# Norm chains through token-major sums, and modulation pieces moved out of the gaps into feed-forward stages

## What is computed

```python
def rms_norm(x, g):
    xf = x.astype(jnp.float32)
    y = xf * lax.rsqrt(jnp.mean(xf * xf, axis=-1, keepdims=True) + RMS_EPS)
    return (y * g.astype(jnp.float32)).astype(x.dtype)
def modulate(x, g_pre, shift, scale):
    return rms_norm(x, g_pre) * (1.0 + scale) + shift
def swiglu(h, w1, w3, w2):
    return (jax.nn.silu(h @ w1) * (h @ w3)) @ w2
def half_ffn(v, shift, scale, gate, g_pre, g_post, w1, w3, w2):
    out = swiglu(modulate(v, g_pre, shift, scale), w1, w3, w2)
    return v + 0.5 * gate * rms_norm(out, g_post)
...
    m_lat = (sc @ w_mod[l] + b_mod[l]).reshape(n_b, N_MOD, 1, D_MODEL)
```

## Time and profile before

| | us |
|---|---|
| median of three runs (2689.0 to 2689.52) | 2689.05 |
| the profiled execution | 2683.14 |
| its span, first to last instruction | 2681.4 |
| PE busy | 2305.6 |
| DVE busy | 1226.1 |
| ACT busy | 816.1 |
| POOL busy | 86.6 |
| mean granted TensorE clock, share of full speed | 0.909 |

### The profile page before, as it was taken

The page is one execution under the profiler, slowest core; times in us unless marked ns, Lnnn a source line. Parts: engine busy times, 40 slices in busy tenths (PEclk is TensorE's granted clock), DMA queues, the critical chain, the costliest instruction groups (busy, mean ns, idle before and its releaser), DMA issues. The chain is left out here.

```text
span 2681.4 us, 29935 instructions
## 1 busy us (share of the span) xinstructions
PE 2305.6 (86%) x12457; PEld 1870.2 (70%) x12457; DVE 1226.1 (46%) x1773; ACT 816.1 (30%) x1248; POOL 86.6 (3%) x99
## 2 busy tenths in 40 slices
PE   4899999799885586899999899999799872877997
PEld 2578888487554575678888578888588551766997
DVE  0422334852546546643334643334644546446555
ACT  1422221532233412242122232222333233313443
POOL 0000000000000310000000000000000000400000
PEclk9899999899787777999999899999889876878998
DMA  7253423422222012342432532432423210025572
GB/s 240 87 144 107 111 75 106 127 89 83 69 63 79 1 48 95 113 107 70 127 89 76 157 89 71 117 97 84 143 73 110 73 63 0 1 63 169 160 196 88
DMA packets 403175, 258.89 MB, mean 97 GB/s; under 512 B 21834, under 2 KB 401760, under 8 KB 403040
## 3 DMA queue, kind: packets, MB, share of 16 engines
q1 hardware_dynamic: 403040, 256.97, 33.0%
HBM read 255.89 MB, written 1.05 MB: 96 GB/s over the span
## 5 line engine op out<-in xcount | busy, mean ns | idle before, releaser
L674 PE MATMUL bank<-uh,wh 128*128 128x512 f32 (+1 forms) x1536 | 565.0, 368 | 38.8 <-DVE ul L1523 25.0
L676 PE MATMUL bank<-uh,wl 128*128 128x512 f32 (+1 forms) x1536 | 558.4, 364 | 0.0
L675 PE MATMUL bank<-ul,wh 128*128 128x512 f32 (+1 forms) x1536 | 558.3, 363 | 0.0
L1468 DVE TENSOR_TENSOR wl<-ring,wh 128x2048 fp32r<-128x2048 f32 (+1 forms) x160 | 323.8, 2023 | 157.2 <-ACT wh L1127 156.4
L1127 ACT ACTIVATE wh<-ring 128x2048 fp32r<-128x2048 f32 (+1 forms) x160 | 270.9, 1693 | 319.4 <-PE bank L676 281.9
L674 PEld LDWEIGHTS bank<-uh,wh 128*128 128x128 f32 x1536 | 293.4, 191 | 99.6 <-issue 41.6
L676 PEld LDWEIGHTS bank<-uh,wl 128*128 128x128 f32 x1536 | 293.6, 191 | 44.9
L675 PEld LDWEIGHTS bank<-ul,wh 128*128 128x128 f32 x1536 | 294.3, 192 | 42.7
L674 PE MATMUL bank<-hh,wh 128*128 128x512 f32 (+1 forms) x704 | 255.4, 363 | 0.0
L675 PE MATMUL bank<-hl,wh 128*128 128x512 f32 (+1 forms) x704 | 255.2, 362 | 0.0
L676 PE MATMUL bank<-hh,wl 128*128 128x512 f32 (+1 forms) x704 | 255.2, 362 | 0.0
(11 more groups left out here) (268 smaller groups left out, 3018.7 us busy)
## 6 DMA issues: line engine op xcount, KB each, us to landing
ring<-in_ffn_w_dram SPq DMA_DIRECT2D x176, 512.0 KB, 5.3
ring<-in_w_mod_dram SPq DMA_DIRECT2D x144, 512.0 KB, 4.6
ring<-in_ffn_w_dram SPq DMA_DIRECT2D x64, 384.0 KB, 3.4
ring<-in_ffn_w_dram SPq DMA_DIRECT2D x64, 320.0 KB, 4.1
ring<-in_w_in_dram SPq DMA_DIRECT2D x40, 512.0 KB, 4.7
ring<-in_w_out_dram SPq DMA_DIRECT2D x16, 512.0 KB, 7.2
ring<-in_w_in_dram SPq DMA_DIRECT2D x4, 544.0 KB, 4.5
ring<-in_w_in_dram SPq DMA_DIRECT2D x2, 1024.0 KB, 5.3
```

The lines of the kernel that those rows point to most:

```text
L674: pe.matmul(bank, w_hi, x_hi, start=first, stop=False)
L675: pe.matmul(bank, w_hi, x_lo, start=False, stop=False)
L676: return pe.matmul(bank, w_lo, x_hi, start=False, stop=last)
L1468: TT(low[:, b, 0:floats], at, high[:, b, 0:floats].bitcast(F32), ALU.subtract).then_inc(wl_ready, 1)
```

## The change

The file has four kinds of edits.

**Where modulation pieces are computed.** The five gap places are gone. There are 9 pieces after up pieces of the first FFN's first part (7 before), 3 after up pieces of its second part, 9 in layer 0's second FFN, 9 in layer 1's first FFN, and 20 and 14 in the mixing blocks (21 and 11 before). In the mixing blocks that is one less at the end of layer 0's, and in layer 1's one more at `mla`, one at `prep` and one at the end.

**The sums and their inverse.** The squares are now the weights of the product and two columns of ones its moving operand: four products of 128 tokens each, two columns wide, per chunk. The sums then lie token by token on the partitions. Root and reciprocal are taken of 128 by 4 values, and `spread` brings the inverse back to 128 by 512 with four products against the identity; DVE reads it from the bank.

**What else a norm chain does.** The gain of postnorm goes to ACT, chunk by chunk while the stage still runs, all but the last before its end; the two gain adds per chunk become one add, and POOL does it for chunks 2 and 5. The last chunk's square goes to PE by itself and not through `yacc`. POOL computes `ul` of the odd chunks, and `wl` of the first piece of each dense stage but the output projection. ACT rounds that first piece at the end of the stage before. `round_in_place` is gone: before `proj` the modulated input is put in a view of the arena and rounded into `uTh` at once.

**The first piece of a stage.** Its 48 products go chunk by chunk over both matrices (in `proj` over both units), so that each chunk of `ul` releases six products and not three.

```diff
-    MOD_PLAN = {("start", 0): 8, ("ffn", 0): 7, ("gap0", 0): 5, ("mix", 0): 21, ("gap1", 0): 5, ("gap2", 0): 5,
-                ("gap0", 1): 5, ("mix", 1): 11, ("gap1", 1): 5}
+    MOD_PLAN = {("start", 0): 8, ("ffn0", 0): 9, ("ffn1", 0): 3, ("mix", 0): 20, ("ffn2", 0): 9,
+                ("ffn0", 1): 9, ("mix", 1): 14}
...
-    MOD_AFTER = {("up0", 0, 0): ("ffn", 0)}
+    MOD_AFTER = {("up0", 0, 0): ("ffn0", 0), ("up1", 0, 0): ("ffn1", 0), ("up0", 0, 1): ("ffn2", 0),
+                 ("up0", 1, 0): ("ffn0", 1)}
...
+        POOL_ADDS = (2, 5)
+        POST_BANK, PRE_BANK, NORM_AT = 5, 4, 56
...
-        MIX_PIECES = ((0, 2, 2, 2, 1, 1, 1, 1, 1, 4), (0, 1, 2, 2, 1, 1, 0, 0, 0, 4))
+        MIX_PIECES = ((0, 2, 2, 2, 1, 1, 1, 1, 1, 3), (0, 2, 2, 2, 1, 1, 1, 0, 0, 5))
...
+            def spread(n, bank, tiles):
+                pe.wait_ge(inverse_ready, n + 1)
+                for i in tiles:
+                    last = pe.matmul(bank[:, i * P:(i + 1) * P],
+                                     rst[:, NORM_AT + i:NORM_AT + i + 1].to_broadcast([P, P]), ident,
+                                     start=True, stop=True)
+                last.then_inc(inverse_spread, 1)
...
+            def token_sums(bank, squares, tiles, first, last):
+                for i in tiles:
+                    done = pe.matmul(bank[:, 2 * i:2 * i + 2], squares[:, i * P:(i + 1) * P], ones[:, 0:2],
+                                     start=first and i == tiles[0], stop=last, skip_group_check=True)
+                return done
...
             def gap(l, j):
-
-                m = gap_pieces(l, j)
-                if m[0]:
-                    mod_work(*m[0])
                 postnorm(l, j)
-                if m[0]:
-                    mod_work(*m[1], banks=(6, 0))
                 if after(l, j)[0] < LAYERS:
                     prenorm(*after(l, j))
-                if m[0]:
-                    mod_work(*m[2])
-                    pe.wait_ge(mod_copied, m[2][0])
...
+                        fresh = part == 0 and j == 0
+                        order = [(g, k) for k in range(KC) for g in range(2)] if fresh else [
+                            (g, k) for g in range(2) for k in range(KC)]
...
+            def split_first(n, floats, parts=(wh, wl)):
+                pool.wait_ge(wh_ready, SPLIT[n] + 1)
+                pool.wait_ge(wl_ready, SPLIT[n])
...
+            def low_rest(l, j, t0, u, high, low):
+                for m in range(1, KC, 2):
+                    pool.wait_ge(uh_ready, split_before(l, j) + m + 1)
+                    G.tensor_tensor(low[:, m, t0:T], u[:, m, t0:T], high[:, m, t0:T].bitcast(F32), ALU.subtract
+                                    ).then_inc(ul_pool, 1)
```

More of the change, by code:

```diff
@@ L636, in mod_work @@
                         mod_turn(g, bank(g))
-            def norm(n, src, blocks, ready, t0):
-                if n:
-                    pe.wait_ge(rms_ready, n)
-                for m in range(blocks):
-                    ready(m)
-                    last = pe.matmul(ps[5][:, t0:T], ones, src(m), start=m == 0, stop=m == blocks - 1)
-                last.then_inc(sums_ready, 1)
-            def prenorm(l, j):
-                t0 = HALF * pre_halves(l, j)[0]
-                norm(6 * l + 2 * j, lambda m: sq[:, m, t0:T], KC,
-                     lambda m: pe.wait_ge(x_squared, 8 * (3 * l + j) + m + 1), t0)
@@ new lines, in token_sums @@
+            def token_sums(bank, squares, tiles, first, last):
[3 more added lines that the diff above has]
+                return done
+            def prenorm(l, j):
+                tiles = tiles_of(pre_halves(l, j))
+                n = 6 * l + 2 * j
+                for m in range(KC):
+                    pe.wait_ge(x_squared, 8 * (3 * l + j) + m + 1)
+                    done = token_sums(ps[PRE_BANK], squares_of(j)[:, m, :], tiles, m == 0, m == KC - 1)
+                done.then_inc(sums_ready, 1)
+                spread(n, ps[PRE_BANK], tiles)
@@ L716, in proj, with product @@
             def proj(l):
-                for n, (kind, j, c0, w, dest) in enumerate(UNITS):
+                def product(n, k):
+                    kind, j, c0, w, dest = UNITS[n]
                     t0 = first_of(l, dest)
@@ L1039, in store @@
             def store():
-                pe.wait_ge(x_ready, 8 * 3 * LAYERS)
+                for m in range(KC):
+                    wait_x(pe, 3 * LAYERS - 1, m)
                 for t in range(2):
@@ L1208, in ffn @@
                             round_piece(PIECES[f"up{part + 1}", l, f][0], 2048)
+                        else:
+                            round_next(l, 2 * f)
+                        if part == PARTS - 1 and j:
+                            gain(l, 2 * f, j - 1, hs)
+                gain(l, 2 * f, KC - 1, hs)
             def proj(l):
@@ L1401, in out_proj @@
                             A(uh[:, m, t0:T], uT[:, m, t0:T], ACT.Copy).then_inc(uh_ready, 1)
+                    for m in range(2 * j - 4, 2 * j - 2):
+                        if m >= 0:
+                            gain(l, 1, m, hs)
+                round_next(l, 1)
+                for m in range(2 * OUT_PIECES - 4, KC):
+                    gain(l, 1, m, hs)
             def store():
@@ L1921, in out_proj @@
                 split_rest(PIECES["out", l][0], 2048)
-                for m in range(KC):
+                for m in range(0, KC, 2):
                     dve.wait_ge(uh_ready, split_before(l, "out") + m + 1)
```

274 lines of the change are left out of this document (161 added, 113 removed).

## The result

| | before | the change |
|---|---|---|
| median of four runs (us) | 2689.03 | 2712.78 |
| lowest and highest | 2670.10 to 2689.52 | 2710.18 to 2716.72 |
| ratio with its 95% interval | | 1.0107 [1.006, 1.0153] |
| profiled execution | 2683.14 | 2714.9 |
| its span | 2681.4 | 2713.1 |

The difference of the two profiled executions is 31.8 us, that of the medians 23.7. The kernel before ran again beside the experiments, with executions from 2680 to 2690 us.

A forecast was written before the change was run, and what follows sets the result against it. PE was busy for 2305.6 of 2681.4 us, so what counted was the gaps between dense stages and what stands there. Pieces +63.4, norm chains -36.4: net +27 us, median from 2689 to 2716, range 2694 to 2729.

The forecast's parts named there:

- The row of pieces: Modulation pieces between up pieces: 23 more pieces and three more first ones, which do not wait, add 63.4 us.
- The 2.92 us: Cost of a modulation piece in a row: 1.07 product, some 0.5 turn, 1.25 waiting for ACT's copy.
- 64 x 0.21 = 13.5 us: Prenorm's token sums in a full gap: 64 narrow passes at 0.21 us, with PE staying at 1.2 GHz.
- The rival from the page's rule: Sustained PE activity raises the clock under the token sums: net -9 us, so 2680; chance 0.09.
- The gaps: Five gaps between dense stages, about 194 us where they were 228; first products 27 to 29 us after the stage.
- The first piece with its hold: First product until PE goes on in a full gap: 14.3 us, the middle of 13.2 and 15.2.
- the upper bound: First piece: POOL's four subtractions of 1.27 us each hold DVE back in full, and PE goes on after 15.2.
- the lower bound: First piece: all 48 products fed together, about 11 at 0.42 and 37 at 0.227 us, make 13.2.
- The modulation pieces in there cost next to nothing where they are.: In the old gaps, pieces standing beside work of DVE and ACT cost next to nothing.
- The start: Start's norm: sums 13.5 for 10, reciprocal and root 0.6 for 4.0, spread +1.9, first piece gains 1.5: 0.
- What was left at nothing: Parts taken at no change, among them the mixing blocks' moved pieces and POOL's hidden split of the first piece.
- Rival 1: Clock rises under the token sums, saving 36 us in gaps and start: net -9, so 2680; chance 0.09.

The follow-up runs named there:

- no_pool: The changed kernel with POOL's two adds and four subtractions of each gap back on DVE; 2710.86 us, ratio 1.0096.
- placement_only: The kernel before with the change's placement of the modulation pieces and nothing of its norm chains; 2729.17 us, ratio 1.0164.
- gaps_again: The changed kernel with its new norm chains, but the modulation pieces where the kernel before had them; 2710.17 us, ratio 1.0085.
- sums_128: The changed kernel with 128 moving columns instead of 2 in each product of the prenorm's token sums; 2686.52 us, ratio 1.0002.
- gaps_128: gaps_again with 128 moving columns in the prenorm's token sums, the edit of sums_128; 2676.66 us, ratio 0.9977.

## Why the prediction was right

- **The row of pieces.** +63.4 forecast, +64.0 measured. The 2.92 us was a period read off the trace in a row with the same queue order, and it holds because that order does not change. Its parts were right too: 1.25 of wait forecast, 1.34 gone when the bank was doubled.
- **The clock in the gap.** "64 x 0.21 = 13.5 us" was 13.8. The step that carried it was to price narrow passes by the products at 2184, which stayed at 0.50 although PE was never idle, and not by the 0.12 they take behind dense work. The rival from the page's rule would have given 2680; the clock did not rise. In the gap at 1530 the errors are small and cancel in part: the sums began at 6.9 us after the stage for 7.8, took 0.3 more than forecast, and ended at 20.7 for 21.3.
- **The gaps.** First products 27.0, 26.7, 27.6, 28.5 and 16.6 us after the stages, forecast 27.1, 27.1, 28.5, 28.5 and 15.5 (order: the gaps at 1115 and 1530, before layer 0's and layer 1's `proj`, with 256 tokens). The first piece with its hold took 14.6, forecast 14.3 as the middle of 13.2 and 15.2. The middle was a choice between two bounds and not worked out: three multiplies were held for 0.94 us each, where the upper bound had four operations of 1.27. no_pool shows the lower bound for what it was, DVE alone: 13.0 to 13.5.
- **"The modulation pieces in there cost next to nothing where they are."** This sentence failed. placement_only shows 12.3 us for 25. It did no harm to the sum, because the new gaps were built up from their own steps and not from the old ones less a saving. But read as "the chains gained 34 us" the sum misleads: 12 of these came from taking the pieces out, 21 from the chains, and gaps_again shows that without the placement the chains lose 22.
- **The start.** 0 forecast (its own terms add to +0.5), +2.6 measured. 2.1 of it is there before the first square: ACT's squares start at 69.38 and not at 67.28, in the set-up that I had not looked at. What delays it was not tried. The norm itself is within 0.5 us.
- **What was left at nothing.** The projections and the last FFN grew by 3.2 us: 1.6 in layer 1's projection, which spent longer at the lower clock (a mean of 0.92 for 0.93), and 1.45 in a wait of a down piece of the last FFN for its low part. The mixing blocks were -1.8 together, -5.9 and +4.1, and the -5.9 is less than they differ by between traces.
- **Rival 1's price.** I gave 36 us to a clock that rises under the sums. sums_128 gave 28 at the start and in the gaps, because the clock is still low for the first 3 to 5 us of them everywhere.

## What to carry to other kernels

Before work is moved beside or away from a chain, find out which engine *is* the chain, before and after the edit: the same five pieces cost 0.5 us each on average beside a chain of DVE and 2.2 each once PE was the chain. A shorter instruction is not a cheaper one if the clock stays down under it: sums with 2 columns moving left PE at 1.2 GHz, and with 64 times the columns they took a third less time. And where a helper is given to every step of a row, look at what the next step waits for in it: a second bank was worth 34.7 us, more than the 33.5 that all edits of the gaps brought.

## What the runs showed of the hardware

- Products with 2 columns moving and 128x128 weights, back to back, took 0.21 us per pass at 1.2 GHz, and the granted clock stayed at 0.50 through 10 us of uninterrupted work; behind dense work they took 0.12. With 128 columns moving the rows of sums in sums_128 started at 0.50 and were at 1.00 3 to 5 us later; in gaps_128 two rows started at 1.00, fell to 0.50 within 0.8 us, and came back. Alternated half and half with products of 512 columns PE stayed at 0.50 for the 26 us of the sums; in the gap with 256 tokens, where the narrow groups were half as long, it rose after some 12.5 us.
- An fp32 pass with 512 columns took 0.92 us at 1.2 GHz, where the split products' passes take 0.43.
- A POOL operation of 1.28 us with two inputs in SBUF made a DVE multiply of 0.40 us, started 0.08 us behind it, take 1.34.
- Layer 0's mixing block took from 390.0 to 406.6 us, up to the first product of `out_proj`, in traces of kernels with the same pieces there, and the fastest had the highest mean granted clock, 0.83 for 0.78 to 0.80. That is as much as many of the edits above are worth.
